# Folding the adaLN accumulators over partitions before TensorE sums them

## The reference

```
ml = split(silu(c)     @ ada_w + ada_b, 9)     # for the latent tokens
mc = split(silu(c_ctx) @ ada_w + ada_b, 9)     # for the context tokens
h  = rms_norm(x) * (1 + scale) + shift ;  x = x + gate * 0.5 * swiglu(h)
```

## Time and profile before

| | |
|---|---|
| median of 3 runs | 1432.85 us (1432.38 to 1434.55) |
| profiled execution | 1431.91 us, of which the span is 1430.2 us |
| TensorE busy | 1401.0 us, 98% of the span |
| VectorE busy | 841.1 us, 59% |
| ScalarE busy | 389.3 us, 27% |
| POOL busy | 634.8 us, 44% |
| one-column sums (L1211) | 160 records, two for each matmul |

### The profile page before, as it was taken

The page is one execution under the profiler, slowest core; times in us unless marked ns, Lnnn a source line. Parts: engine busy times, 40 slices in busy tenths (PEclk is TensorE's granted clock), DMA queues, the critical chain, the costliest instruction groups (busy, mean ns, idle before and its releaser), DMA issues.

```text
span 1430.2 us, 21249 instructions
## 1 busy us (share of the span) xinstructions
PE 1401.0 (98%) x8528; PEld 1249.5 (87%) x8528; DVE 841.1 (59%) x1290; ACT 389.3 (27%) x716; POOL 634.8 (44%) x399
## 2 busy tenths in 40 slices
PE   7999999999999999999999999999999999999997
PEld 3599999999999899897887888888898899999996
DVE  2774466558546446317556349924777856655566
ACT  3320010011001011014635141124123345455455
POOL 1362443534534434432541318633756556556552
PEclk9999999999999999999999999999999999999999
DMA  9532353335245234223312268375664333434422
GB/s 349 171 108 67 119 137 119 118 86 170 72 124 159 78 123 150 78 53 98 85 49 52 68 194 234 124 223 170 204 177 126 90 109 90 118 89 113 123 70 79
DMA packets 235646, 177.58 MB, mean 124 GB/s; under 512 B 33273, under 2 KB 210589, under 8 KB 235549
## 3 DMA queue, kind: packets, MB, share of 16 engines
q1 hardware_dynamic: 216368, 145.65, 35.2%
q10 hardware_dynamic: 19180, 30.58, 6.6%
HBM read 156.83 MB, written 19.37 MB: 123 GB/s over the span
## 4 chain that ended last, share of the span: by engine, by line
PE 87%; DVE 8%; ACT 2%; issue 1%; DMA 1%; SPq 0%; DVEq 0%; ACTq 0%
PE ps L1114 42%; PE ps L1729 13%; PE ps L1369 9%; PE ps L1790 5%; PE ps L1372 4%; PE ps L1146 2%; PE ps L1123 2%; PE ps L1463 2%; PE ps L1321 1%; PE ps L1202 1%; PE ps L1211 1%; DVE ada_acc L2516 1%; PE ps L1606 1%; DVE h_lo L3253 1%; PE ps L1570 1%
## 5 line engine op out<-in xcount | busy, mean ns | idle before, releaser
L1036 POOL TENSOR_SCALAR w_hi<-w_raw 128x1024 fp32r<-128x1024 f32 x129 | 150.8, 1169 | 620.8 <-PE ps L1114 341.4
L1039 POOL TENSOR_TENSOR w_lo<-w_raw,w_hi 128x1024 fp32r<-128x1024 f32 x129 | 321.2, 2490 | 10.8
L1114 PE MATMUL ps<-h_hi,w_lo 128*128 128x384 f32 (+2 forms) x1000 | 291.5, 351 | 0.6 <-DVEq L3024 0.6
L1114 PE MATMUL ps<-h_hi,w_hi 128*128 128x384 f32 (+2 forms) x1000 | 287.7, 347 | 0.0
L1114 PE MATMUL ps<-h_lo,w_hi 128*128 128x384 f32 (+2 forms) x1000 | 287.3, 347 | 0.0
L1114 PEld LDWEIGHTS ps<-h_hi,w_lo 128*128 128x128 f32 x1000 | 179.6, 189 | 16.6 <-issue 4.9
L1114 PEld LDWEIGHTS ps<-h_hi,w_hi 128*128 128x128 f32 x1000 | 181.5, 188 | 10.6
L1114 PEld LDWEIGHTS ps<-h_lo,w_hi 128*128 128x128 f32 x1000 | 181.3, 188 | 10.1
L1096 POOL TENSOR_TENSOR w_lo<-w_raw,w_hi 128x512 fp32r<-128x512 f32 x90 | 115.4, 1296 | 105.3 <-ACT w_hi L2291 103.7
L2516 DVE SCALAR_TENSOR_TENSOR ada_acc<-ada_w,cs,ada_acc 128x1024 f32<-128x1024 f32 x70 | 109.7, 1599 | 10.5 <-DMA ada_w<-in_ada_w_dram 8.4
L1933 ACT ACTIVATE silu<-ps 128x768 f32<-128x768 f32 (+1 forms) x26 | 20.3, 780 | 323.9 <-PE ps L1114 314.8
(11 more groups left out here) (416 smaller groups left out, 2909.1 us busy)
## 6 DMA issues: line engine op xcount, KB each, us to landing
w_raw<-in_ffn_w_gate_dram SPq DMA_DIRECT2D x44, 512.0 KB, 5.0
w_raw<-in_ffn_w_up_dram SPq DMA_DIRECT2D x44, 512.0 KB, 4.0
w_raw<-in_ffn_w_down_dram SPq DMA_DIRECT2D x44, 512.0 KB, 4.3
ada_w<-in_ada_w_dram ACTq DMA_DIRECT2D x32, 512.0 KB, 4.1
w_raw<-in_w_in_dram SPq DMA_DIRECT2D x32, 512.0 KB, 4.1
ada_w<-in_ada_w_dram SPq DMA_DIRECT2D x30, 512.0 KB, 4.7
c_scr<-cp ACTq DMA_DIRECT2D x16, 288.0 KB, 4.0
b_scr<-bt_sb ACTq DMA_DIRECT2D x16, 256.0 KB, 4.1
```

What stands on the lines that cost most here:

```text
L1036: pool.tensor_scalar(w_hi[:, s, 0:cols], w_raw[:, s, 0:cols], 1.0, 1.0, ALU.mult, ALU.mult)\
L1039: pool.tensor_tensor(w_lo[:, s, 0:cols], w_raw[:, s, 0:cols], w_hi[:, s, 0:cols].bitcast(F32), ALU.subtract).then_inc(w_split, 1)
L1114: last = pe.matmul(mv[2], st, mv[part], start=(first and q == 0), stop=(n == len(terms) - 1 and q == 2))
```

## The change

After the last tile of a group the accumulator is folded twice, so that fewer partitions hold the parts of one sum. In the first fold ScalarE copies partitions 64 to 127 of the first vector and partitions 0 to 63 of the second one (or of the second half of the columns, where there is one vector) to the other half of the partitions in a buffer `fold_sb`, and VectorE adds: now partitions 0 to 63 hold the first vector and 64 to 127 the second. The second fold does the same between quarters of 32 partitions and halves of the columns. `fold_ones` is a 128 x 4 matrix with a block of ones of 32 rows in each column: one stationary piece of 128 columns then gives four columns of results. 16 matmuls become 4, and 8 become 2. `fold_sb` lies on the buffer `gu`.

A fold is a chain: copies (ScalarE), adds (VectorE), copies, adds; only then does `folded` release TensorE. The instructions go into the written order of each engine (in the diff, indented lines that are not marked are context):

```diff
             def ada_sums(cols, g):
-                for t in range(KD):
-                    for v in range(ada_vecs(g)):
-                        last = pe.matmul(cols[:, t, v:v + 1], ada_vec(g, v)[:, P * t:P * t + P], ones[:, 0:1],
-                                         start=True, stop=True)
+                pe.wait_ge(folded, folds_made(g))
+                n = FOLD_BLOCKS
+                for t in range(fold_width(g) // FOLDS // P):
+                    last = pe.matmul(cols[:, n * t:n * t + n], ada_vec(g, 0)[:, P * t:P * t + P], fold_ones[:, :],
+                                     start=True, stop=True)
                 return last
...
+            def fold_copies(g):                                   # ScalarE
+                act.wait_ge(acc_ok, ada_added(g, KD))
+                if g > ADA_START:
+                    act.wait_ge(folded, folds_made(g - 1))
+                t, w = ada_vec(g, 0), fold_width(g)
+                other = ada_vec(g, 1) if ada_vecs(g) == 2 else t[:, w:D]
+                act.activation(fold_sb[0:64, 0:w], t[64:P, 0:w], ACT.Copy)
+                act.activation(fold_sb[64:P, 0:w], other[0:64, 0:w], ACT.Copy).then_inc(fold_copied, 1)
+
+            def fold_copies_again(g):
+                act.wait_ge(folded, folds_made(g) - 1)
+                t, w = ada_vec(g, 0), fold_width(g) // 2
+                for r in (0, 64):
+                    act.activation(fold_sb[r:r + 32, 0:w], t[r + 32:r + 64, 0:w], ACT.Copy)
+                    last = act.activation(fold_sb[r + 32:r + 64, 0:w], t[r:r + 32, w:2 * w], ACT.Copy)
+                last.then_inc(fold_copied, 1)
...
+                        if part.segs + i == 0 and f == 2:
+                            g0 = ADA_START if n == NT else ADA_MIX + 1
+                            fold_copies(g0)
+                            fold_copies_again(g0)
...
                     if n == NT and ADA_START < g < ADA_MIX:
                         ada_tile(g, KD - 1)
+                        fold_copies(g)
+                        fold_copies_again(g)
...
             for k in range(KD):
                 wo_square(k)
+                if k == 3:
+                    fold_copies(ADA_MIX)
+                elif k == 4:
+                    fold_copies_again(ADA_MIX)
...
+            def fold(g):                                          # VectorE
+                dve.wait_ge(fold_copied, folds_made(g) - 1)
+                t, w = ada_vec(g, 0), fold_width(g)
+                other = ada_vec(g, 1) if ada_vecs(g) == 2 else t[:, w:D]
+                TT(t[0:64, 0:w], t[0:64, 0:w], fold_sb[0:64, 0:w], ALU.add)
+                TT(t[64:P, 0:w], other[64:P, 0:w], fold_sb[64:P, 0:w], ALU.add).then_inc(folded, 1)
+
+            def fold_again(g):
+                dve.wait_ge(fold_copied, folds_made(g))
+                t, w = ada_vec(g, 0), fold_width(g) // 2
+                for r in (0, 64):
+                    TT(t[r:r + 32, 0:w], t[r:r + 32, 0:w], fold_sb[r:r + 32, 0:w], ALU.add)
+                    last = TT(t[r + 32:r + 64, 0:w], t[r + 32:r + 64, w:2 * w], fold_sb[r + 32:r + 64, 0:w], ALU.add)
+                last.then_inc(folded, 1)
...
                             for k in ((2,), (6,), (), ())[f_]:
                                 ada_add(ADA_MIX + 1, k)
+                            if f_ == 2:
+                                fold(ADA_MIX + 1)
+                                fold_again(ADA_MIX + 1)
...
                             if f_ == 2:
+                                fold(ADA_START)
                                 s5_powers()
+                                fold_again(ADA_START)
...
                             ada_add(ADA_START + nth, KD - 1)
+                        if ada_here_now and k == 4:
+                            fold(ADA_START + nth)
+                        if ada_here_now and k == 5:
+                            fold_again(ADA_START + nth)
...
+                if k == 4:
+                    fold(ADA_MIX)
+                elif k == 5:
+                    fold_again(ADA_MIX)
```

More of the change, by code:

```diff
@@ L153, in ada_added, with fold_width, folds_made @@
     return sum(KD * ada_vecs(q) for q in range(ADA_START, g)) + k * ada_vecs(g)
+FOLDS = 2
+FOLD_BLOCKS = 2 * FOLDS
+FOLD_ROWS = P // FOLD_BLOCKS
+def fold_width(g):
+    return D if ada_vecs(g) == 2 else D // 2
+def folds_made(g):
+    return FOLDS * (g - ADA_START + 1)
 def ada_acc0(g):
@@ L372, in build @@
     cs = place("cs", [P, KD, 2], F32)
+    fold_ones = place("fold_ones", [P, FOLD_BLOCKS], F32)
     eps = place("eps", [P, 1], F32)
@@ L387, in build @@
     silu = place("silu", [P, 2, NT], F32)
+    fold_at = top[0]
     gu = place("gu", [P, 2, NT], F32)
+    fold_sb = place("fold_sb", [P, D], F32, at=fold_at)
     ssq = place("ssq", [P, NT], F32)
@@ L599, in ada_vec, with ada_sum_cols @@
         return ada_acc[:, v + ada_acc0(g), :]
+    def ada_sum_cols(j):
+        return lat(j)[:, ADA_COL:ADA_COL + 2 * KD]
     def ada_late(j):
-        return ctx_(j)[:, 0:2 * KD].rearrange("p (t v) -> p t v", v=2)
+        return ctx_(j)[:, 0:2 * KD]
     ADA_COL = 384
@@ L652, in build @@
         acc_ok = sem("acc_ok")
+        fold_copied = sem("fold_copied")
+        folded = sem("folded")
         consts = sem("consts")
@@ L1348, in seg @@
                         if two and g and v == (1 if nth else 2 * tiles - 1):
-                            pe.wait_ge(acc_ok, ada_added(g, KD))
-                            last = ada_sums(ada_cols(j, ADA_COL), g)
+                            last = ada_sums(ada_sum_cols(j), g)
                         if not two and nth == 0 and v == 2 * tiles - 1:
-                            pe.wait_ge(acc_ok, ada_added(ADA_MIX + 1, KD))
                             last = ada_sums(ada_late(j), ADA_MIX + 1)
@@ L2363, in _ @@
             dve.memset(nsgn[64:128, :], -1.0).then_inc(consts, 1)
+            link(dve.memset(fold_ones[:, :], 0.0))
+            for b in range(FOLD_BLOCKS):
+                dve.memset(fold_ones[FOLD_ROWS * b:FOLD_ROWS * b + FOLD_ROWS, b:b + 1], 1.0)
             dve.sem_inc(s5_in_used, 1)
@@ L2521, in ada_bias, with sums_bias @@
                 return TT(mod[:, t, 0:n], cols[:, :, 0:n], vt[:, t].unsqueeze(2).to_broadcast([P, KD, n]), ALU.add)
+            def fold(g):
[11 more added lines that the diff above has]
+                last.then_inc(folded, 1)
+            def sums_bias(cols, g):
+                t = slice(KD * g, KD * g + KD)
+                if ada_vecs(g) == 2:
+                    for v in range(2):
+                        last = TT(mod[:, t, v].rearrange("p (h t) -> p h t", h=2),
+                                  cols[:, :].rearrange("p (t v h) -> p v h t", v=2, h=2)[:, v, :, :],
+                                  vt[:, t].rearrange("p (h t) -> p h t", h=2), ALU.add)
+                    return last
+                return TT(mod[:, t, 0].rearrange("p (h t) -> p h t", h=4), cols[:, 0:KD].rearrange("p (t h) -> p h t", h=4),
+                          vt[:, t].rearrange("p (h t) -> p h t", h=4), ALU.add)
             def scale_cols(q, g_row):
```

9 lines of the change are left out of this document (4 added, 5 removed).

## The result

The changed kernel takes 1440.15 us (median of 5 runs, 1437.86 to 1440.87), the kernel before 1433.9 (5 runs, 1432.38 to 1435.32). The ratio is 1.0035, with a 95% interval of 1.0022 to 1.0048: slower, by 5.0 us as the ratio has it, 6.3 as the medians do. The forecast was +4.2 us and 1437.0. The profiled executions stand further apart: the span grew from 1430.2 to 1439.1 us, +8.9. The profiled execution of before (1431.91 us) was faster than all five that its median is taken from, and the one of after (1440.87) was the slowest of its five.

What follows compares the result with a forecast made beforehand. TensorE, busy 1401.0 of 1430.2 us, was taken as the bound. Savings at groups 3 to 6 against stalls at 2, 7 and 8 gave +4.2 us: 1431.9 to 1436.1, plus 0.9 for the median, 1437.0; 8-in-10 range 1429 to 1442.

Steps and rivals of the forecast that it cites:

- g = 2, wait and records: Group 2's sums: TensorE stalls 5.9 us for second adds queued behind s5_powers, then runs eight records; net +3.2 us.
- g = 2, clock behind it: After group 2's sums: the stall brings a low clock losing 1.8 us, as was lost there before; net 0.
- g = 3 (records, clock): Group 3's sums: 24 fewer records save 2.6 us, and the low clock there goes, saving 3.4 us.
- g = 4, 5, 6: Sums of groups 4, 5 and 6: fewer records, folds hidden; -2.6 us at 4, -2.6 at 5 and 6 together.
- g = 7, wait and records: Group 7's sums: TensorE stalls 3.2 us for the fold chain, then runs four records; net +1.9 us.
- g = 7, clock: After group 7's sums: no low clock was forecast, 0 us.
- g = 8, wait and records: Group 8's sums: no slack, folds behind tile subtractions and held by POOL's SBUF instructions; net +8.5 us.
- g = 8, clock: After group 8's sums: a stall of 7 to 10 us brings the low clock, +1.8 us.
- rival A: Group 8's fold meets no POOL instruction, clock stays up after it: no change, 1432.5 us; decided by chain under 7 us; chance 0.27.
- C: Stalls at groups 2, 7 and 8 are half those forecast, through overlap and less POOL: 1425.7 us; chance 0.10.
- D: TensorE never waits at any group, 120 records and both low clocks gone: 1414.5 us; chance 0.05.
- rival B: Low clock after stalls costs 3.4 us at groups 2 and 8, and comes at 7 too: +5.0, 1442 us; chance 0.13.

Runs made afterwards that it cites:

- e_burst: a_3to6 with each matmul of the folded sums issued four times: 1434.28 us, ratio 1.0011 to the kernel before.
- a_3to6: Changed kernel folding only groups 3, 4, 5 and 6, old one-column sums elsewhere: 1423.28 us, ratio 0.9922 to the kernel before.
- d_fill: Changed kernel with unused matmuls filling TensorE's three waits, 84 of them at group 2: 1436.89 us, ratio 1.0018 to the kernel before.
- i_fill54: Changed kernel with unused matmuls filling TensorE's three waits, 54 of them at group 2: 1433.48 us, ratio 1.0005 to the kernel before.
- b_2ahead: Changed kernel with group 2's second fold ahead of s5_powers on VectorE instead of behind it: 1442.7 us, ratio 1.0057 to the kernel before.
- c_no8: Changed kernel without the fold of group 8, which has its one-column sums again: 1431.09 us, ratio 0.9978 to the kernel before.
- g_8first: Changed kernel with group 8's folding adds ahead of the four tile additions on VectorE: 1442.21 us, ratio 1.0068 to the kernel before.
- k_apart: Kernel before, no fold, sums of groups 2 and 3 split eight matmuls ahead of a product and eight behind: 1431.46 us, ratio 0.9982.
- m_apart3: Kernel before, no fold, sums of groups 2, 3 and 4 split eight matmuls ahead of a product and eight behind: 1426.88 us, ratio 0.9953.
- l_best: Against the kernel before: groups 3 to 6 folded twice, 7 once, 8 unfolded, group 2's unfolded sums split round a product: 1422.05 us, ratio 0.9924.
- h_456: Changed kernel folding only groups 4, 5 and 6, one-column sums elsewhere: 1426.47 us, ratio 0.9961 to the kernel before.

## Why the prediction was right, and where a size was off

The median came out 3.2 us above the forecast, inside the range, and on the side that had most of the chance. The mechanism was right; that the number came so near is in part luck, as the terms show. Taken apart with the trace after (all of g = 2, 7 and 8 up to the next product, against the 3.49, 1.75 and 1.77 us of the old sums):

| term | forecast | measured |
|---|---|---|
| g = 2, wait and records | +3.2 | 6.35 + 1.73 - 3.49 = +4.6 |
| g = 2, clock behind it | 0 | 2.8 - 1.8 = +1.0 |
| g = 3 (records, clock) | -2.6 - 3.4 | -2.6 - 3.4 |
| g = 4, 5, 6 | -5.2 | -5.2 |
| g = 7, wait and records | +1.9 | 3.52 + 0.82 - 1.75 = +2.6 |
| g = 7, clock | 0 | +3.0 |
| g = 8, wait and records | +8.5 | 7.89 + 0.88 - 1.77 = +7.0 |
| g = 8, clock | +1.8 | +2.4 |
| sum | +4.2 | +9.4 (spans: +8.9) |

The clock terms are half of the time at 0.50 behind the sums: 129.2 to 134.9, 1047.0 to 1053.0, 1120.0 to 1124.7.

By these terms the forecast was 5.2 us too low: 6.3 for the clock, less 1.1 for the waits, of which the one of g = 8 was 2.0 us shorter than forecast. Against the ratio (+5.0) it was only 0.8 too low, and 2.1 against the medians (+6.3). A likely reason for the rest, which the forecast did not have, is in the base. The execution of the kernel before from which the terms were read was a fast one: its mean clock was 0.994, where the median of the kernel's runs beside the experiments was 0.992 in three sets of four. By an estimate from these two clocks, 0.002 of 1430 us, such a run loses 3 us more than the profile before shows; the forecast had added 0.9.

- What the change takes: right. 40 records at 0.11 us; the far end (4-column records dearer) didn't come. The low clock of g = 3 went with its burst, and e_burst brings one back with the burst and nothing else, though of 1.8 us in the execution profiled.
- The hidden folds at g = 3 to 6: right, shown by a_3to6 (-11.2 us of -11.2).
- The three waits: right in place and cause (5.9, 3.2 and 9.9 forecast, 6.35, 3.52 and 7.89 measured). The largest was over-sized: I had POOL's next pair beside the second fold, but POOL waits for TensorE's sums there (1120.32), so it can't be in the way of what TensorE waits for. Only the first add was held, 0.7 us. The chain of g = 8, 8.04 us, was nevertheless above the 7 us that rival A named, and a clock fall followed: A is out. So are C (half the waits) and D (none), by the lengths of the waits.
- The mis-sized term is the low clock behind the waits: forecast 1.8 us more than before, measured 6.4 behind the sums and 1.7 in them, since their records took twice 0.11 us. This is the mechanism of rival B; the wait of g = 7, 3.5 us long, brought it too. The forecast had no fall of the clock at g = 7, only B had, and by the prediction's own signs that counts against it. The filled waits (d_fill, i_fill54) show that it is the idling, and not the fold or the bursts, that lowers the clock: same chains, clock 1.00, 4.3 us less by the ratios and 6.7 by the medians. B's price, 3.4 us a place, is about right here: 3.7, 3.4 and 2.8 us at g = 2, 7 and 8, with what the sums themselves lost. At g = 7 it is 1.8 in the profiled executions of b_2ahead, c_no8 and g_8first. B's sum has an error: with a forecast of 0 at g = 7 its 3.4 us add 3.4 there and not 1.8, so B stood for 6.6 us more than the forecast and not 5.0, 1443.6 us and not 1442. Measured were 6.3 more for the clock in this execution.
- My reading of the burst was right and too narrow. I took the fall at g = 3 for a thing of that place, and the trace's 1.00 at g = 4 for an exemption. A burst of the same length at g = 4 does bring the low clock in the profiled executions of e_burst and k_apart, and setting it apart too gave m_apart3 its further gain. What decides whether a burst brings it in a given execution is not shown.

## What to carry to other kernels

Before TensorE's work is moved to another engine, ask at each site separately whether the result is ready when TensorE comes: here the same fold is worth 11.2 us at four sites with cover and costs 16 (by the ratios) to 21 us (by the terms) at three without. The waits of 3.4 to 9.1 us that these runs put in front of TensorE had 1.7 to 3.7 us lost to the half clock with them, so such a wait is to be priced with that too. A long run of matmuls with few moving columns can cost clock as well as records (at g = 3 3.5 us of records, and 1.8 or 3.4 us in clock). Setting it in two pieces round dense work adds no instruction, where the operand is ready one product sooner, and gave 6.7 us here. And a forecast that starts from one profiled execution takes over that execution's luck with the clock.

## What the runs showed of the hardware

- A profiled execution's low clocks are a sample. The kernel before ran between 1430.8 and 1437.7 us here, and its 23 runs beside l_best have mean clocks of 0.995 (the fastest, 1431.48 us) to 0.990 (the slowest, 1436.89). A 0.91 in 680 to 700 (1.8 us) is in some kernels' executions and not in others, though nothing of that stretch is changed.
- The low clocks of a busy TensorE come in two sizes: 0.91 over 20 us, 3.6 us at half rate and 1.8 lost (g = 3 in h_456 and e_burst), or 0.83 and 3.4 lost (g = 3 before; 3.3 at g = 4 in k_apart). A burst of this length at the same place brought either, or none (g = 4 before). k_apart's began at 395.07, and the clock fell near 397.8, with TensorE busy throughout.
- ScalarE's copies from partitions 64 to 127 into 0 to 63 cost what one in place does (0.63 us for 512 columns, 1.06 for 1024, on 64 partitions), and 32 partitions are no cheaper than 64 or 128. Adds in a row on changing partition ranges start behind the end of the one ahead (124.67, 125.36, 126.05, 126.75, with 0.68 us each), where instructions on all 128 partitions start about 0.1 us before it (two products of s5_powers at 121.52 and 121.86, 0.42 us each). The Trainium skill, page "VectorE: DVE Perf Modes", section "Two Vector instructions with no wait between them", has a rule for it: an instruction is held until every earlier VectorE instruction has finished where an input or the output starts in another group of 32 partitions than that of the last instruction that read, or wrote, the same memory. The trace agrees.
